# Tokens laid out by class modulo 16 for a dilated attention stage, with one dilation's probabilities turned by VectorE

## What is computed

```
q, k = partial_rope(rmsnorm(proj q, k))      # per kind
s    = q k / 8, allowed: same class modulo dilation, causal, within the window
o_g, lse_g = softmax(s) v, log of the denominator
o    = sum over g of softmax(lse)_g * o_g, then o @ w_out
```

## Time and profile before

| | |
|---|---|
| median of 3 runs | 1622.22 us (1621.16 to 1622.39) |
| the profiled execution's own time | 1617.19 us |
| its span | 1615.1 us |
| TensorE, VectorE, ScalarE, GpSimd busy | 96%, 59%, 43%, 28% |
| granted TensorE clock | 0.996 of full speed |
| moved by DMA | 173.49 MB, mean 107 GB/s |

### The profile page before, as it was taken

One profiled execution on the slowest core, in us unless ns is written; L12 is line 12 of the kernel. 1 busy time (PEld: TensorE's weight loads), 2 busy tenths in 40 slices (PEclk: granted clock), 3 DMA queues, 4 the chain that ended last, 5 costly groups with the idle time before them and its releaser, 6 DMA issues.

```text
span 1615.1 us, 23549 instructions
## 1 busy us (share of the span) xinstructions
PE 1556.6 (96%) x8666; PEld 1294.7 (80%) x8674; DVE 954.7 (59%) x1644; ACT 692.4 (43%) x1148; POOL 447.2 (28%) x608
## 2 busy tenths in 40 slices
PE   7999988999999999899999999999988999999998
PEld 6776655888888887799988888998766888888886
DVE  4456566557474748544547576554655457575748
ACT  6433332255453545444434334443442353545453
POOL 3412200020111631262527465443822120101110
PEclk9999999999999999999999999999999999999999
DMA  6221110457565664432222412222232377575753
GB/s 173 81 64 40 53 40 1 157 130 176 137 167 143 159 153 80 131 87 72 72 82 68 132 53 66 79 69 64 66 119 92 118 156 197 115 189 122 183 126 81
DMA packets 111355, 173.49 MB, mean 107 GB/s; under 512 B 13216, under 2 KB 45984, under 8 KB 111008
## 3 DMA queue, kind: packets, MB, share of 16 engines
q1 hardware_dynamic: 91664, 134.51, 26.8%
q0 software_dynamic: 17408, 33.56, 12.8%
q10 hardware_dynamic: 2192, 4.20, 0.7%
HBM read 165.89 MB, written 6.36 MB: 107 GB/s over the span
## 4 chain that ended last, share of the span: by engine, by line
PE 74%; DVE 10%; POOL 6%; issue 4%; ACT 3%; DMA 1%; SPq 1%; ACTq 0%; DVEq 0%; POOLq 0%
PE ps L562 50%; PE ps L834 15%; PE ps L620 3%; POOL qrs L1643 3%; PE ps L652 2%; POOL qss L1642 2%; DVE pT_sb L1319 2%; PE ps L664 1%; PE ps L634 1%; DVE qss L1230 1%; DVE w_l L1452 1%; PE ps L593 1%; ACT w_h L910 1%; ACT sq L951 1%; DMA raw<-in_mlp_w 1%
## 5 line engine op out<-in xcount | busy, mean ns | idle before, releaser
L562 PE MATMUL ps<-w_h,act_h 128*128 128x512 f32 x768 | 317.4, 413 | 8.9 <-DVE w_l L1197 3.4
L562 PE MATMUL ps<-w_h,act_l 128*128 128x512 f32 x768 | 307.0, 400 | 0.0
L562 PE MATMUL ps<-w_l,act_h 128*128 128x512 f32 x768 | 305.9, 398 | 0.0
L562 PEld LDWEIGHTS ps<-w_h,act_h 128*128 128x128 f32 x768 | 192.1, 250 | 28.2 <-issue 11.5
L562 PEld LDWEIGHTS ps<-w_l,act_h 128*128 128x128 f32 x768 | 192.2, 250 | 16.0
L977 ACT ACTIVATE p_sb<-ps,negmax 128x128 f32<-128x128 f32 (+3 forms) x256 | 93.4, 427 | 260.0 <-DVE negmax L1278 195.0
L562 PEld LDWEIGHTS ps<-w_h,act_l 128*128 128x128 f32 x768 | 193.0, 251 | 14.3
L562 PE MATMUL ps<-act_h,w_h 128*128 128x512 f32 x512 | 199.8, 390 | 0.9 <-DVE w_l L1423 0.9
L562 PE MATMUL ps<-act_h,w_l 128*128 128x512 f32 x512 | 199.2, 389 | 0.0
L562 PE MATMUL ps<-act_l,w_h 128*128 128x512 f32 x512 | 199.2, 389 | 0.0
L834 PE MATMUL ps<-w_h,op_h 128*128 128x512 f32 x448 | 175.1, 391 | 0.0
(11 more groups left out here) (195 smaller groups left out, 2598.7 us busy)
## 6 DMA issues: line engine op xcount, KB each, us to landing
w_raw<-in_dil_w_in SPq DMA_DIRECT2D x72, 512.0 KB, 3.7
raw<-in_mlp_w SPq DMA_DIRECT2D x64, 512.0 KB, 4.7
raw<-in_mlp_w POOLq DMA_DIRECT2D x48, 512.0 KB, 5.9
w_raw<-in_mlp_w SPq DMA_DIRECT2D x32, 512.0 KB, 5.0
w_raw<-in_fox_w_in SPq DMA_DIRECT2D x22, 512.0 KB, 3.6
p_sb<-in_mlp_w SPq DMA_DIRECT2D x16, 512.0 KB, 5.4
pT_sb<-in_mlp_w SPq DMA_DIRECT2D x16, 512.0 KB, 6.7
w_raw<-in_mlp_w POOLq DMA_DIRECT2D x16, 512.0 KB, 6.9
```

What stands on the lines that cost most here:

```text
L562: return mm(ps_out, lhs[i], rhs[j], start=(k == 0 and term == 0), stop=(k == KT - 1 and term == 2))
```

## The change

The host hands x over in another order and puts the output rows back. Within each tile of 128 natural tokens the rows lie by residue modulo 4, in it by class modulo 16, in it by time. The norm's preparation spreads each tile's columns at a stride of four, so that the columns of act are blocks of 128 for a residue modulo 4, in them 32 for a class modulo 16. Kinds 1 and 2, and q and k of kind 0, read plain blocks. Only v of kind 0 reads every fourth column, and ScalarE's evacuation writes kind 0's q and k to their places by tile. Masks follow the new order: they are made in parts and put in order by a matmul of a permutation, then copied by VectorE. In kind 2 the probabilities are diagonal blocks of 32x32, which VectorE turns from SBUF to SBUF; TensorE's transposes and the copy from PSUM are left out there.

```diff
-LAYOUT = {0: 0, 1: 1, 2: 1}
+NC = 4
+def turned_by_pe(s):
+    return SETS[s][0] != 2
+def turned_count(a):
+    return sum(turned_by_pe(set_of(b)) for b in range(a + 1))
...
 def tok(act, k, tile, every_fourth):
+    if not every_fourth:
         return act[:, k, tile * P:(tile + 1) * P]
+    return act[:, k, :].rearrange("p (m t) -> p t m", t=NT)[:, tile, :]
...
 def prep_dst(n, half, t):
+    if n == 3:
+        c = slice(4 * half, 4 * half + 4)
+        return [x[:, c, :].rearrange("p k (m t) -> p t k m", t=NT)[:, t, :, :] for x in (act_h, act_l)]
...
 # SyncE: reorder, positions
-sp.dma_start(acc_dram.rearrange("(p r) c -> p r c", r=NT), acc12...)
+sp.dma_start(acc_dram.rearrange("(r p) c -> p r c", r=NT), acc12...)
-               acc_dram.rearrange("(t p) c -> p t c", p=P))
+               acc_dram.rearrange("(p t) c -> p t c", p=P))
-sp.dma_start(pos_i[:, 0, :], positions[0].rearrange("(t p) -> p t", p=P), allow_slow_non_contiguous=True)
...
 # TensorE
 def turn_probs(s, a):
+    if not turned_by_pe(s):
+        return
...
 if proj == 2 and b == 1 and k == 0 and term == 0:
+    mm(ps_s[1][:, 0:2 * P], block_rows, by_time, start=True, stop=True)
     mm(ps_s[0][:, 0:NT], spread, place[:, :], start=True, stop=True).then_inc(turned_full, 1)
+last = token_bank(B, k, term, b % 4, kind == 0 and b >= QK_SET)
 # forget_gates, b == 3
+pe.wait_ge(pool_done, 1)
+mm(ps_s[1][:, 0:3 * P], class_rows[:, :], class_masks...).then_inc(masks_full, 1)
...
 # ScalarE: qk_evacuate
+if kind == 0:
+    dst = dst[:, :, :].rearrange("p i (t r m) -> p r i m t", t=NT, r=NT)[:, b % 4, :, :, :]
+    src = src.rearrange("p i (m t) -> p i m t", t=NT)
...
 # ScalarE: probs
 act.wait_ge(max_done, a + 1)
-if a >= 2:
-    act.wait_ge(pt_full, a - 1)
+if a >= 2 and turned_by_pe(set_of(a - 2)):
+    act.wait_ge(pt_full, turned_count(a - 2))
+elif a >= 2:
+    act.wait_ge(pt_done, a - 1)
...
 # VectorE: norm_turned
+v.tensor_copy(causal[:, :], ps_s[1][:, 0:P])
+v.tensor_copy(residue[:, :], ps_s[1][:, P:2 * P])
 v.tensor_copy(xss[:, 4, :], ps_s[0][:, 0:NT])
...
 # VectorE: probs_back
-dve.wait_ge(pt_full, a + 1)
+if not turned_by_pe(s):
+    dve.wait_ge(exp_done, a + 1)
+    dve.wait_ge(pv_done, a - 1)
+    v.transpose(pT_sb[:, a % 2, :], p_sb[:, a % 2, :]).then_inc(pt_done, 1)
+    return
+dve.wait_ge(pt_full, turned_count(a))
...
 # VectorE: forget_gates, b == 4
+dve.wait_ge(masks_full, 1)
+v.tensor_copy(causal[:, :], ps_s[1][:, 0:P])
+v.tensor_copy(banded[:, 0:P], ps_s[1][:, P:2 * P])
+v.tensor_copy(banded[:, P:2 * P], ps_s[1][:, 0:P])
+v.tensor_copy(upto_t[:, :], ps_s[1][:, 2 * P:3 * P]).then_inc(masks_done, 1)
...
 # GpSimd: tables, once for one layout instead of for two
-for lay in range(2):
-    for hlf in range(2):
+for hlf in range(2):
...
 # kernel(): the host's order
+order = np.arange(S).reshape(NT, P // NT // NC, NC, NT)
+rows, places = order.transpose(0, 3, 2, 1).reshape(S), order.transpose(2, 1, 0, 3).reshape(S)
+laid["x"] = np.asarray(inputs["x"])[:, rows]
+laid["positions"] = np.asarray(inputs["positions"])[:, places]
```

More of the change, by code:

```diff
@@ L199, in out_fill, with set_of @@
     return range(3 * i, 3 * i + 3) if 0 <= i < NT else range(0)
+def turned_by_pe(s):
+    return SETS[s][0] != 2
+def set_of(a):
+    return max(s for s in range(len(SETS)) if TICK0[s] <= a)
+def turned_count(a):
+    return sum(turned_by_pe(set_of(b)) for b in range(a + 1))
 def out_early(a):
@@ L246, in trunk @@
                 ones_t = sb("ones_t", [P, P], F32, first)
+                class_rows = sb("class_rows", [P, P], BF16, first)
+                class_masks = sb("class_masks", [P, 3, P], BF16, first)
                 b_f = sb("b_f", [P, NH], F32, first)
@@ L293, in trunk @@
         tab_b = sb("tab_b", [P, 6, NT, ROT])
-        pos_i = sb("pos_i", [P, 2, NT], I32)
-        pos_f = sb("pos_f", [P, 2 * NT])
+        pos_i = sb("pos_i", [P, NT], I32)
+        pos_f = sb("pos_f", [P, NT])
         freq = sb("freq", [P, HALF])
-        ang = sb("ang", [P, 2 * NT, HALF])
-        turns = sb("turns", [P, 2 * NT, HALF])
-        sin_t = sb("sin_t", [P, 2 * NT, HALF])
+        ang = sb("ang", [P, NT, HALF])
+        turns = sb("turns", [P, NT, HALF])
+        sin_t = sb("sin_t", [P, NT, HALF])
         sinh_t = turns
@@ L429, in mlp_unit, with norm_slot @@
             return i * PER_CHUNK + (BANK_MLP[layer] + p)
-        def norm_slot(s):
+        def norm_slot(s, value=False):
             kind = SETS[s][0]
-            return 0 if kind == "fox" else 2 if LAYOUT[kind] == 0 else 4
+            return 0 if kind == "fox" else 2 if kind == 0 and value else 4
         def wait_bank_free(pe, B):
@@ L567, in weights_ready, with token_bank @@
                     pe.wait_ge(wl_done, more + (B + k // 2 + 1))
-            def token_bank(B, k, term, tile, layout=0, out=False):
+            def token_bank(B, k, term, tile, every_fourth=False, out=False):
                 slot = (B // 4 * 4 + k // 2) % WR
@@ L576, in token_bank @@
                 a_h, a_l = (hid_h, hid_l) if out else (act_h, act_l)
-                return product(ps_proj[B % 2][:, :], k, term, (tok(a_h, k, tile, layout), tok(a_l, k, tile, layout)),
+                return product(ps_proj[B % 2][:, :], k, term, (tok(a_h, k, tile, every_fourth), tok(a_l, k, tile, every_fourth)),
                                (w_h[slot][:, k % 2, :], w_l[slot][:, k % 2, :]))
@@ L743, in forget_gates @@
                 if b == 10:
[L745 removed]
+                    pe.wait_ge(masks_done, 1)
                     pe.wait_ge(softplus_done, 3)
@@ L759, in terms @@
                     for m in range(first, end):
-                        last = token_bank(B0 + b, m // 3, m % 3, b % NT, 0, True)
+                        last = token_bank(B0 + b, m // 3, m % 3, b % NT, False, True)
                     if end == 3 * KT:
@@ L1590, in _ @@
             out_projection(BANK_FOX_OUT, 1)
-            v.tensor_reduce(quad[:, :], ident[:, :].rearrange("p (j r) -> p j r", r=NT), AX, ALU.add)
-            v.tensor_reduce(place[:, :], ident[:, :].rearrange("p (j r) -> p r j", r=NT), AX, ALU.add).then_inc(quad_done, 1)
+            v.tensor_reduce(quad[:, :], ident[:, :].rearrange("p (r j) -> p j r", r=NT), AX, ALU.add)
+            v.tensor_reduce(place[:, :], ident[:, :].rearrange("p (r j) -> p r j", r=NT), AX, ALU.add).then_inc(quad_done, 1)
             mlp(0)
@@ L1756, in _ @@
             pool.wait_ge(consts_done, 1)
[L1757 to L1761 removed]
+            back, ahead = [[-1, NT], [-NC, NC], [-16, 8]], [[1, NT], [NC, NC], [16, 8]]
+            link(g.memset(class_rows[:, :], 0.0))
+            select(class_rows[:, :].rearrange(BY_CLASS, r=NT, c=NC), back, 0, 1, ALU.not_equal, 1.0)
+            link(g.memset(class_masks[:, 0:2, :], 0.0))
+            link(g.memset(class_masks[:, 2, :], -1.0))
+            select(class_masks[:, 0, :].rearrange(BY_CLASS, r=NT, c=NC), back, 0, 1, ALU.is_ge, NEG)
+            select(class_masks[:, 1, :].rearrange(BY_CLASS, r=NT, c=NC), ahead, 0, -1, ALU.is_ge, NEG)
+            select(class_masks[:, 2, :].rearrange(BY_CLASS, r=NT, c=NC), ahead, 0, -1, ALU.is_ge, 0.0)
             link(g.memset(pick[:, :], 0.0))
@@ L1836 @@
     r = run_bass_kernel_spmd(nc, [arrays], core_ids=[0])
-    return r.results[0]["out_0"]
+    out = np.empty((1, S, D), np.float32)
+    out[:, rows] = r.results[0]["out_0"]
+    return out
```

76 lines of the change are left out of this document (38 added, 38 removed).

## The result

| | before | after |
|---|---|---|
| median | 1621.14 us (1619.48 to 1622.39, 8 runs) | 1629.12 us (1626.83 to 1631.69, 8 runs) |
| the profiled execution's own time | 1617.19 us | 1631.17 us |
| its span | 1615.1 us | 1629.1 us |
| granted TensorE clock | 0.996 | 0.990 |

A forecast was written before the change was run, and what follows sets the result against it. TensorE, busy 96%, was taken to bound the kernel, with a GpSimd cycle close behind beside kind 2. -13.0 + 11.2 + 1.0 + 1.4 + 0.6 = +1.2 us gave a 1623.4 us median, range 1613.5 to 1632.5.

The forecast's parts named there:

- The wait and its cycle: Kind 2 ticks: exponentials wait for VectorE's turn, cycle 1.0 us longer, about 8.7 us; +11.2 us with strided value banks included.
- The turn: VectorE's turn of kind 2's probabilities, taken as 0.68 us like the copy; bounds 0.4 and 1.3 us.
- The scattered evacuation: ScalarE writes kind 0's q and k every 512 bytes, 16 times, 10 in the cycle: +1.0 us (0 to +3.5).
- value banks: Kind 0's value banks go from plain to strided: 4 in each of two sets, 0.29 us each, counted in their steps.
- The plain blocks: Kinds 1 and 2: 48 strided banks become plain, 0.29 us saved each, less 0.9 us of waits: -13.0 us.
- Preparation and masks: Dilated norm: strided preparation +1.4 us (0 to +3); two more VectorE mask copies before the first rotation +0.6 us (0 to 0.9).
- The last stretch: Last banks, last attention step and output: +0.6 us, for two strided banks in the last attention step.
- (a): Kind 2 ticks: the wait does not lengthen the cycle; -8.9 us, 1613.3 us; chance 0.20.
- (b): Same cycle in kind 2: turn or strided evacuation is dear, ten times the excess over 0.68 and 0.71 us; 1630 us; chance 0.27.
- (c): Strided blocks: no saving, the moving operand sets the pace; +14.2 us, 1636 us; chance 0.03.

The follow-up runs named there:

- wait alone: Kernel before, only kind 2's exponentials made to wait for VectorE's copy of the probabilities two ticks back, not TensorE's transposes: 1633.59 us, ratio 1.0066 to before.
- plain write: Kernel after, with ScalarE writing kind 0's q and k in plain blocks, their reordering left out: 1625.52 us, ratio 1.0027 to before.
- other order: Kernel after, kind 0's q and k evacuated to the same places by reading PSUM at stride four and writing runs of 32: 1626.65 us, ratio 1.0039 to before.
- late and in order: Kernel after, VectorE turning tick a-1 last in its tick, and kind 0's q and k written in runs of 32: 1606.68 us, ratio 0.9917 to before.
- late: Kernel after, with VectorE turning tick a-1, not a-2, at the end of its tick: 1609.37 us, ratio 0.9931 to before.
- turn first: Kernel after, with VectorE turning tick a-2 ahead of the maxima of tick a: 1615.16 us, ratio 0.9953 to before.
- plain preparation: Kernel after, with the norm's preparation ahead of the dilated layer writing plain blocks, order by class left out: 1624.96 us in one run.
- TensorE's turns: Kernel after, with TensorE again turning kind 2's probabilities: 1612.56 us, ratio 0.9938 to before.

## Why the prediction came out as it did

The median, 1629.12 us, lies inside the stated range of 1613.5 to 1632.5 and outside the forecast's own 1620 to 1628. The mechanism is the one that was forecast; its size was put too low. The forecast had +1.2 us against before, the medians give +8.0, and in the table of stretches no row came out below its forecast: the terms did not make up for each other.

**The wait and its cycle: right, in mechanism and size.** The forecast had the exponentials start behind the turn, GpSimd's add come every 8.7 us and TensorE show gaps. The kernel before with that wait alone gives 8.71 us, and the kernel after with the scattered write mended gives 8.73 (8.83 with the plain write). How often it counts was put too low for set 7. With the wait alone its three ticks from bank 1 to 4 take 26.07 us, 8.69 each, as forecast. But the step to bank 7 is 4.9 us longer, not 4.0: the intervals before and behind them grew by 0.5, 0.6, 0.3 and 0.3 us.

**The turn: right.** 0.70 us measured where 0.68 was taken. The Trainium skill's figure (VectorE: DVE Perf Modes, "The three transpose paths") had led to an estimate of 0.75; the trace is close to it. How 311 ns for one block became 0.75 us for four, the prediction does not show.

**The scattered evacuation: the term that was mis-sized.** I took 0.1 us each and 0.35 as upper bound, from a strided read on VectorE. It costs 0.47 us (1.17 against 0.70 in the same lines), above the bound. The nearest row was of another engine and of the other side of the access. Ten times 0.37 us is 3.7 us, and the two steps beside kind 2 came out 2.3 and 1.3 above their forecast, 3.6 together. That these agree is in part chance. With the evacuation short the two steps are 2.2 us (plain order) and 3.4 us (other order) shorter than in after, and in the whole time the ratio falls from 1.0051 to 1.0027 or to 1.0039, 3.9 or 1.9 us. So the term is worth some 2 to 4 us where 1.0 was taken, and even with a short evacuation the two steps stay above the forecast for wait and value banks, 10.6 us: they are 12.9 and 11.8 us longer than in before. The rule on 16-byte lines (the Trainium skill, Advanced Engine Details and Errata, "Memory Cachelines") pointed this way, and I gave it too little weight; it agrees with the trace also in that the same elements written as runs of 32 cost nothing.

**The plain blocks: right in kind, a little less.** I said 3.5 us for each of three steps and 2.6 for that of set 2. By the adds it was 2.98 (set 3), 2.97 (set 5), 2.94 (set 6) and 1.2 (set 2). A bank thus saves 0.25 us and not 0.29, and of set 2's 3.0 us 1.8 were lost again. In that step TensorE's turns wait 2.8 us for GpSimd's rotation, where it was 1.3:

```profile
PE ps L693 <- POOL qn L1707: 2.8, 5, 1.2
```

Together the plain blocks gave 10.1 us of the 13.0. The weight load by itself would have promised far more: beside kind 1 a strided load took 0.31 us before and a plain one takes 0.19 after, 0.12 us times 24 in a bank. The loads overlap the matmuls, and less than a tenth of that is seen in the bank's pace.

**Preparation and masks: right.** +1.7 for 1.4, and +0.6 for 0.6.

**The last stretch: right, but for the clock of one execution.** It is 3.4 us longer, not 0.6. In three windows (1170 to 1185, 1185 to 1200, 1240 to 1260 us) TensorE's clock falls to 0.97, 0.92 and 0.91, shown in the last section; 15 x 0.03 + 15 x 0.08 + 20 x 0.09 = 3.5 us of work at full speed are missing, in a stretch where the kernel before shows 1.00. The other profiled executions bear this out. For each I summed, over windows of 5 us from bank 7's add to the second mark, the window's length times what its granted clock lacks to 1.00. Four of them miss nothing and are 0.6, 0.7, 0.9 and 1.0 us longer than before there (late and in order, late, plain write, other order). Four miss 1.7 us and are 1.4 to 1.9 us longer (turn first, plain preparation, wait alone, TensorE's turns). After misses 3.4 us and is 3.4 us longer. So the value banks cost about what was forecast, and most of this row is not the change's own price. No run sets the clock by itself.

**The rivals.** (a), that the wait costs nothing, falls with the wait alone. (b), dear turn or dear evacuation, holds in half: the evacuation, not the turn. Its condition, over 0.2 us together above my values, was met: +0.02 and +0.37. By its own rule, ten times these, it would give +5.1 us against before. That 1629.1 us comes out nearly at the 1630 I gave it is luck: that figure was made with a turn of 1.2 us and an evacuation of 0.9, and the smaller saving of the plain blocks fills the gap. (c), no saving on plain blocks, falls: the steps of sets 3, 5 and 6 are 3.0 us shorter each, and with TensorE turning, the kernel is 0.6% faster than before.

What I did not say: the two halves of the change hurt each other. In the kernel with TensorE's turns the slow evacuation costs nothing measurable in the tick, because the factor arguments end later. I had counted the evacuation as in the cycle at any rate, in rival (a) too. It is there only in the kernels in which VectorE turns: in after behind the wait, and with the turn first or late because the factor arguments then end before it.

## What to carry to other kernels

Before work moves from a full engine to one with idle time, write down the cycle of buffers and queues that the new producer closes: what matters is where in its queue the releasing instruction stands, and what stands behind the one that waits. Here the same instruction costs 1.1% against TensorE's turns (1.0051 to 0.9938) or nothing that the whole time shows (0.9931), by its place in VectorE's tick. Where ScalarE's evacuation must scatter on one side, scatter the read from PSUM and keep the write in runs (0.71 against 1.17 us here), and time such an access by a row of the same engine and the same side. Before a difference of some us in one profiled execution is given a cause, look whether other executions with the same instructions there show it too.

## What the runs showed of the hardware that was not expected

**Scattered writes and scattered reads are not alike on ScalarE.** An evacuation of 128x512 float32 from PSUM takes 0.70 us plain, 0.706 us when it reads PSUM with a stride of four elements, and 1.17 us when it writes SBUF with neighbours in time 512 bytes apart. Writing at a stride of 16 bytes in the preparation takes 1.10 us against 0.59.

**TensorE's clock fell in and behind stretches with short gaps.** Stretches of after; the third number from the end of a line is the granted clock:

```profile
1120.00:1200.00 80.00, 71.63 (x436) 57.88 (x435) 42.22 (x86) 35.02 (x72) 47.47 (x69) 0.94 0.28 88
...
1139.00:1148.00 9.00, 6.06 (x30) 4.76 (x32) 5.48 (x11) 3.68 (x11) 6.17 (x10) 0.92 0.20 58
1148.00:1157.00 9.00, 9.00 (x56) 7.26 (x54) 6.42 (x13) 3.68 (x10) 6.14 (x10) 0.70 0.23 61
...
1170.00:1185.00 15.00, 12.57 (x66) 10.76 (x65) 7.34 (x14) 6.16 (x9) 12.56 (x17) 0.97 0.28 86
1184.00:1193.00 9.00, 9.00 (x40) 7.69 (x40) 2.29 (x5) 3.12 (x5) 1.72 (x3) 0.81 0.57 187
1185.00:1200.00 15.00, 15.00 (x73) 12.94 (x72) 4.32 (x8) 6.01 (x10) 0.72 (x2) 0.92 0.60 201
1240.00:1260.00 20.00, 17.75 (x106) 13.86 (x105) 9.70 (x19) 5.40 (x8) 3.77 (x6) 0.91 0.45 148
```

The kernel before, in which TensorE idles 3.6 of the same 80 us and not 8.4, has 1.00 there and in the last of those stretches:

```profile
1120.00:1200.00 80.00, 76.38 (x536) 59.81 (x536) 47.88 (x98) 34.12 (x74) 46.29 (x66) 1.00 0.31 100
1240.00:1260.00 20.00, 20.00 (x98) 16.48 (x97) 11.63 (x14) 6.16 (x9) 0.00 (x0) 1.00 0.51 172
```

A mean of 0.94 over 80 us means that for some 12% of them the clock stood at 1.2 and not 2.4 GHz. From 1139 to 1148 TensorE idled 2.94 of 9 us; in the next 9 us it has no gap and a mean clock of 0.70. From 1184 to 1193 again it has none and runs at 0.81. My reading is that gaps were paid for beyond their own length; no run tests it by itself. The dips show in the kernel with the wait alone as well (0.98 in the same 80 us) and not in the one with the turn late and the write in order (1.00, with 5.8 us idle). How much TensorE idles does not settle it: from 830 to 905 us the kernel with the write in the other order idles 7.1 us at a mean clock of 0.95, after 10.8 us at 0.98, and the kernel with the wait alone 5.4 us at 1.00.

**GpSimd's selects with a three-part pattern are slower.** The 32 selects over 128x128 in the MLP chunk took 22.6 us from the first start to the last end, 0.71 each, and 15.1 before with a plain pattern, 0.47 each. They lie beside TensorE's work, and the weight transfers issued behind them on the same queue came at their old distance again by the second one; no time was lost.
